# Per-token scales spread to all partitions by two transfers through memory in place of a matmul of ones with a diagonal

## What is computed

```python
def rmsnorm(x, g):
    y = x * rsqrt(mean(x * x, axis=-1) + RMS_EPS)
    return y * g

# first block: mixers, then the feed-forward part
x = x + concatenate([y_a, y_b, y_c]) @ w_out
h = rmsnorm(x, norm_ffn)
up = dwconv3(h @ ffn_w_up, ffn_conv_w, ffn_conv_b)     # 2048 -> 2 * 5632, width-3 convolution over tokens
gate, val = split(up, 2)
x = x + (silu(gate) * val) @ ffn_w_down                # 5632 -> 2048
x = rmsnorm(x, norm_final)

# second block: attention with a forget gate, then an MLP
h = rmsnorm(x, norm_g[0])
q, k, v, f_pre = split(h @ fox_w_in)                   # 2048 -> 3 * 2048 + 16
...
x = x + rmsnorm(attention @ fox_w_out, norm_g[1])
x = x + rmsnorm(square(relu(rmsnorm(x, norm_g[2]) @ mlp_w1)) @ mlp_w2, norm_g[3])
```

## Time and profile before

| | |
|---|---|
| median of 3 runs | 2156.41 us (2156.26 to 2156.44) |
| span of the profiled execution, first to last instruction | 2154.2 us |
| mean granted TensorE clock | 0.999 |
| PE busy | 2146.4 us, 100% of the span as printed |
| DVE / ACT / POOL busy | 1304.1 / 1010.3 / 63.3 us |
| share of PE in the chain that ended last | 98% |
| DMA | 412.43 MB, mean 191 GB/s |

### The profile page before, as it was taken

How to read it: one execution, slowest core, us unless ns; L and a number is a source line. 1 busy time by engine, 2 the same in 40 slices (tenths; PEclk the granted TensorE clock), 3 DMA queues, 4 the chain that set the end, 5 groups by cost and what they waited for, 6 DMA issues and landing times.

```text
span 2154.2 us, 28093 instructions
## 1 busy us (share of the span) xinstructions
PE 2146.4 (100%) x11745; PEld 1862.1 (86%) x11745; DVE 1304.1 (61%) x1610; ACT 1010.3 (47%) x1188; POOL 63.3 (3%) x85
## 2 busy tenths in 40 slices
PE   9999999999999999999999999999999999999999
PEld 7888888888888888888898889888888888888887
DVE  7968557777777775444755665466555555444445
ACT  6444446555545554444655444445434334444443
POOL 3030000000000000000001010000000000000000
PEclk9999999999999999999999999999999999999999
DMA  9655656565655555555566555547666665555552
GB/s 343 212 169 176 217 188 201 182 195 189 196 189 184 194 176 203 192 194 193 166 211 201 157 177 189 198 142 215 186 187 194 186 189 193 195 195 196 192 192 105
DMA packets 269214, 412.43 MB, mean 191 GB/s; under 512 B 7013, under 2 KB 247589, under 8 KB 250400
## 3 DMA queue, kind: packets, MB, share of 16 engines
q1 hardware_dynamic: 266080, 398.48, 56.8%
q0 software_dynamic: 2432, 11.75, 1.5%
q10 hardware_dynamic: 576, 0.40, 0.1%
HBM read 408.49 MB, written 2.11 MB: 191 GB/s over the span
## 4 chain that ended last, share of the span: by engine, by line
PE 98%; DMA 1%; ACT 1%; DVE 0%; SPq 0%; issue 0%; ACTq 0%; DVEq 0%
PE bank L1586 35%; PE bank L1599 18%; PE bank L1647 11%; PE bank L1648 11%; PE bank L1652 11%; PE bank L1589 2%; PE bank L1601 2%; PE bank L1590 2%; PE bank L1481 1%; DMA M<-in_xt 1%; PE bank L1673 0%; PE bank L1670 0%; PE bank L1671 0%; PE bank L1564 0%; PE bank L1531 0%; PE bank L1517 0%
## 5 line engine op out<-in xcount | busy, mean ns | idle before, releaser
L822 DVE TENSOR_TENSOR wlo<-raw,whi 128x2048 fp32r<-128x2048 f32 (+1 forms) x372 | 852.5, 2294 | 762.1 <-ACT whi L496 762.0
L496 ACT ACTIVATE whi<-raw 128x2048 fp32r<-128x2048 f32 (+1 forms) x371 | 710.2, 1916 | 777.9 <-PE bank L1652 421.3
L1586 PE MATMUL bank<-hh,whi 128*128 128x512 f32 x3360 | 807.3, 392 | 0.1
L1586 PEld LDWEIGHTS bank<-hh,whi 128*128 128x128 f32 x3360 | 618.2, 188 | 123.3 <-issue 0.9
L1599 PEld LDWEIGHTS bank<-hh,wlo 128*128 128x128 f32 x3360 | 430.6, 191 | 16.9 <-DVE wlo L822 0.6
L1599 PE MATMUL bank<-hh,wlo 128*128 128x256 f32 x3360 | 436.0, 283 | 0.2 <-DVE wlo L822 0.2
L1647 PE MATMUL bank<-whi,hh 128*128 128x512 f32 x1072 | 417.3, 389 | 0.0
L1648 PE MATMUL bank<-whi,hh 128*128 128x512 f32 x1072 | 417.1, 389 | 0.0
L1652 PE MATMUL bank<-wlo,hh 128*128 128x512 f32 x1072 | 264.8, 389 | 0.0
L1652 PEld LDWEIGHTS bank<-wlo,hh 128*128 128x128 f32 x1072 | 201.2, 188 | 41.9
L1647 PEld LDWEIGHTS bank<-whi,hh 128*128 128x128 f32 x1072 | 201.2, 188 | 41.8 <-DVE M L894 0.2
(11 more groups left out here) (249 smaller groups left out, 935.8 us busy)
## 6 DMA issues: line engine op xcount, KB each, us to landing
raw<-in_mlp_w SPq DMA_DIRECT2D x128, 1024.0 KB, 5.5
raw<-in_ffn_w_up SPq DMA_DIRECT2D x88, 1024.0 KB, 5.1
raw<-in_ffn_w_down SPq DMA_DIRECT2D x44, 1024.0 KB, 4.8
raw<-in_fox_w_in SPq DMA_DIRECT2D x32, 1024.0 KB, 5.3
raw<-in_w_in SPq DMA_DIRECT2D x31, 1024.0 KB, 5.6
raw<-in_fox_w_in SPq DMA_DIRECT2D x16, 1032.0 KB, 5.4
raw<-in_w_out SPq DMA_DIRECT2D x16, 1024.0 KB, 4.8
raw<-in_fox_w_out SPq DMA_DIRECT2D x16, 1024.0 KB, 4.7
```

The costliest lines, as they stand in the source:

```text
L496: e.activation(whi[i % RING][:, 0:n], raw[i % RAW][:, 0:n], ACT.Copy).then_inc(s_hi, 1)
L822: e.tensor_tensor(wlo[i % RING][:, 0:n], raw[i % RAW][:, 0:n], whi[i % RING][:, 0:n].bitcast(F), ALU.subtract).then_inc(s_lo, 1)
L1586: e.matmul(bank[b][:, :], wh[:, k, s], hh[:, kk, :], start=kk == 0, stop=False)
```

## The change

For `r_up` and `rtot` the diagonal, the matmul and the copy are gone. Instead POOL writes the two columns of 128 words to a row of `cum` in HBM (two transfers), waits for both, and reads the row back to all 128 partitions of `rb` (one transfer). DVE waits for that transfer where it waited for the matmul. The early use (`rstd`) stays.

```diff
-    51: [("up_r", 0), ("split", 55)], 53: [("up_r_out", 0)], U_DOWN - 2: [("early", 1)],
-    182: [("gains", 0)], 183: [("gain_squares", 0)], 184: [("both_r", 0)], 185: [("ahead", 188)], 186: [("both_r_out", 0)],
+    51: [("up_r", 0), ("split", 55)], U_DOWN - 2: [("early", 1)],
+    182: [("gains", 0)], 183: [("gain_squares", 0)], 184: [("both_r", 0)], 185: [("ahead", 188)],
...
+            def to_all(n, r):
+
+                for h in range(2):
+                    e.dma_start(cum[n:n + 1, h * P:h * P + P].rearrange("o p -> p o"), r[:, h:h + 1]).then_inc(s_rdram, 16)
+                e.wait_ge(s_rdram, 32 * (n + 1))
+                e.dma_start(rb[:, :], cum[n, :].partition_broadcast(P)).then_inc(s_rall, 16)
...
             e.dma_start(gfr, A["gf_row"].partition_broadcast(P)).then_inc(s_gainf, 16)
+            e.wait_ge(s_rcp, 3)
+            to_all(0, r_up)
             e.wait_ge(s_xg, 2)
+            e.wait_ge(s_rr, 3)
+            to_all(1, rtot)
             e.wait_ge(s_unit, U_FOX + 4)
...
                 e.tensor_tensor(rtot, r_b, r_a, ALU.mult).then_inc(s_rr, 1)
-                e.wait_ge(s_rr, 3)
-                diagonal(rtot)
...
                         root(3, SS[0], 1.0 / D, RMS_EPS, r_up)
-                        e.wait_ge(s_rcp, 3)
-                        diagonal(r_up)
...
                 if g == 0:
-                    spread_out(2)
+                    e.wait_ge(s_rall, 16)
                 conv(kind, j, b, group_done(U_UP, g))
...
                 if (kind, j) == ("k", 0):
-                    spread_out(3)
+                    e.wait_ge(s_rall, 32)
                     out_of_psum("q", 0, group_done(U_FOX, 0))
...
-                    elif what == "up_r_out":
-                        e.wait_ge(s_lx, 32)
-                        spread(2)
-                    elif what == "both_r_out":
-                        e.wait_ge(s_lx, 48)
-                        spread(3)
...
                     elif what == "sums":
+                        e.wait_ge(s_lx, 48)
                         e.wait_ge(s_gt, 12)
```

More of the change, by code:

```diff
@@ L273, in two_block_program @@
         s_ss, s_red, s_rr, s_dg, s_bc, s_rb = (sem(n) for n in ("s_ss", "s_red", "s_rr", "s_dg", "s_bc", "s_rb"))
+        s_rdram, s_rall = sem("s_rdram"), sem("s_rall")
         s_gainf, s_gain1, s_gain3, s_xt, s_xg, s_yg = (sem(n) for n in ("s_gainf", "s_gain1", "s_gain3", "s_xt", "s_xg", "s_yg"))
@@ L859, in diagonal, with spread_out @@
                     e.tensor_scalar(dg[:, h, :], ident[:, :], r[:, h:h + 1], None, ALU.mult).then_inc(s_dg, 1)
-            def spread_out(n):
-                e.wait_ge(s_bc, n)
+            def spread_out():
+                e.wait_ge(s_bc, 1)
                 e.tensor_copy(rb[:, :], bank[7][:, 0:T]).then_inc(s_rb, 1)
-                e.wait_ge(s_rb, n)
+                e.wait_ge(s_rb, 1)
             def root(n, sums, scale, eps, dst):
@@ L1245, in vector @@
             convolved("v", 0, 2, group_done(U_IN, 1))
-            spread_out(1)
+            spread_out()
             times_r("x1", 0)
@@ L1440, in turn_two, with spread @@
                         t.then_inc(s_xt, 1)
-            def spread(n):
-                e.wait_ge(s_dg, 2 * n)
+            def spread():
+                e.wait_ge(s_dg, 2)
                 e.matmul(bank[7][:, 0:T], ones, dg[:, :, :].rearrange("p h t -> p (h t)"), start=True, stop=True).then_inc(s_bc, 1)
@@ L1486, in side @@
                     if what == "spread":
-                        spread(1)
-                    elif what == "up_r_out":
-                        e.wait_ge(s_lx, 32)
-                        spread(2)
-                    elif what == "both_r_out":
-                        e.wait_ge(s_lx, 48)
-                        spread(3)
+                        spread()
                     elif what == "filter1":
@@ L1700, in last_rows @@
                 e.wait_ge(s_yg, 8 + 8)
-                e.wait_ge(s_dg, 7)
+                e.wait_ge(s_dg, 3)
                 for n, c in enumerate(BY_DIAGONAL):
@@ L1744, in tensor @@
             rows(1, [up_free(n_up + 1, 0), up_free(n_up + 1, 1), up_free(n_up + 2, 0), up_free(n_up + 2, 1), up_free(n_up, 0), up_free(n_up, 1),
-                     None, (s_rb, 2)])
+                     (s_lx, 32), (s_lx, 32)])
             def fox_free(g, n):
```

## The result

| | before | changed |
|---|---|---|
| median | 2156.26 us (2156.17 to 2156.44, 5 runs) | 2175.88 us (2173.63 to 2177.04, 5 runs) |
| ratio, with 95% interval | | 1.0089 [1.0079, 1.01] |
| span of the profiled execution | 2154.2 us | 2174.1 us |
| granted TensorE clock | 0.999 | 0.996 |
| waits of PE in the two places | 0 | 8.1 + 7.3 us |

A forecast was written before the change was run, and what follows sets the result against it. PE was taken as the bound from end to end; 0.86 us saved against waits of 0.2 and 0.5 gave -0.16 us, so 2156.41 became 2156.25, say 2156.3 us. The range was 2155.4 to 2160.5.

The forecast's parts named there:

- PE is the bound; the two matmuls are worth 0.86 us: Whole span: PE bounds end to end; each removed spread saves 0.43 us, in up and attention projections, together 0.86.
- The form of L: Both places, finished factor to `rb` landed: POOL notices 0.29, issue 0.54, write 4.7, read 4.5; L = 10.0, range 8.3 to 12.8.
- The write, 4.7 us: Both places: second write's issue to the read's issue, 4.7 us, from `fox_b2` landing in 4.4 plus 0.3; low 3.88.
- my upper end of 7.3: Both places: highest price for the write, from the 3 KB `skip_row`, which landed in 7.0 us.
- writes of single words are slow: Rival, 12%: POOL's wait for both writes lengthens; write 7.3, read 4.9, L 13.0, net 5.8, time 2162.2 us.
- 2L - 20.2: Net change in us once L exceeds 9.8 (up) and 9.5 (attention), each microsecond costing PE one per place; passes 4.3 at 12.2.
- The read, 4.5 us: Both places: read of the row to 128 partitions lands in 4.5 us, like `mask`; low 3.6, high 4.7.
- The free lateness, 3.3 to 4.0 us in the up projection and L = 9.5 in the attention projections: Lateness before PE waits: up 3.3 (unit 57) or 4.0 (unit 56), allowing L = 9.8; attention, q0's bank, L = 9.5.
- a wait for `whi` of 56: Up projection: this wait would show the line of work wrong; unit 57 was expected, with under 1 us.
- The clock isn't priced: PE's clock: no cost for a fall, since it stayed at 1.00 with 1.24 us idle in ten; shorter waits expected.
- DVE holds up POOL's transfers: Rival, 3%: both places, DVE's `wlo` instructions delay the second write's descriptors; PE waits 4.9 and 5.1, time 2165.6 us.

The follow-up runs named there:

- experiment 7: Changed kernel, same six transfers, but groups 0 and 1, q0 and k0 are emptied first and multiplied by `rb` later: 2155.51 us, ratio 0.9996.
- experiment 3: Changed kernel, but each write sends a 512-byte row of ones from one partition instead of a column of 128 words: 2159.02 us, ratio 1.0014.
- probes: Kernel before, with single transfers of various piece sizes and spacings added that nothing waits for; 128 words side by side landed in 9.4 to 10.0 us.
- Experiment 5: Kernel before, without any transfer, but the matmul for `r_up` two units later, behind unit 55 instead of 53: 2165.43 us.
- Experiment 2: Changed kernel, but words written 8 bytes apart, 2 KB read to every partition and every second word copied to `rb` by DVE: 2169.22 us.
- second kernel of experiment 3: Changed kernel with row writes, but the read to 128 partitions takes an input row instead of the row just written: 2159.11 us.

## Why the prediction was wrong, step by step

- **PE is the bound; the two matmuls are worth 0.86 us**: right. In the changed kernel the low parts of units 53 and 54 start 5.57 apart (335.90 and 341.47) instead of 6.00. With the waits out of the way (experiment 7) the median is 0.8 below before, which the interval doesn't separate from nothing. (Of PE's waits before, the 1.1 us at line 1612 that I counted as one wait is two, of which the longer took 0.9; nothing hangs on it.)
- **The form of L**: right. POOL's 0.28 and 0.54, then write, then read, just as the chain shows.
- **The write, 4.7 us**: the step that failed. It took 11.2 and 9.5 from its issue to the read's, above my upper end of 7.3. The 4.7 is what the write of a row took at the first place (experiment 3). I took the duration from `fox_b2` and called a read with rows of 128 bytes the nearest row of the trace. The probes say what was wrong with that: rows don't matter, bytes don't, but a write whose pieces start 4 bytes apart isn't like anything that the kernel had done before. The rival "writes of single words are slow" named the mechanism, its place and the point from which it decides; it was given 12% and, with a wrong bound for the write (and 4.9 for the read, which no row shown gives), 2162.2. Its 2L - 20.2, with the two measured L, is 15.5, and the measured waits less the 0.86 are 14.5.
- **The read, 4.5 us**: too low by 2. It measured 6.7 and 6.4 there, and 6.5 and 6.2 with an input row. I had taken the landing of `mask`, beside which one load of weights was pending at a time, and here there were two (experiment 3). By itself this term would have cost what experiment 3 measured, 2.7 us, and stayed within the range.
- **The free lateness, 3.3 to 4.0 us in the up projection and L = 9.5 in the attention projections**: right. In the up projection DVE starts at 351.06, 12.15 late when the run's own shift of 0.41 is taken off; less the 4.0 for `whi` of unit 56 that is 8.15, and 8.06 were measured. The sign that the prediction gave for this line of work being wrong, a wait for `whi` of 56, was a wrong sign: unit 57 has the smaller margin (3.3 against 4.0), but PE comes to unit 56 first, so any lateness above 4.0 shows there, and only the difference of 0.7 is left for unit 57. In experiment 3 both are seen, 1.57 and 0.40. In the changed kernel the 0.7 went by unseen, since unit 56 ran 1.96 us longer. In the attention projections 17.0 - 9.5 = 7.5, and 7.3 were measured. Experiment 5 has the same relation without transfers.
- **The clock isn't priced**: a second step that failed, and it followed from the first. It rested on 1.24 us of idle time. Behind waits of 8.1 and 7.3 us PE came back at 1.2 GHz, and that cost 1.96 and 2.63 us, 4.6 of the 19.6. Experiment 2 had waits of 4.8 and 4.3 us and lost 2.1 and 2.5 behind them; the single-word rival, with waits of 3.2 and 3.5, left the term out too.
- **DVE holds up POOL's transfers**: not supported. In experiment 3, with DVE and POOL in the same order, the writes take 4.4 and 3.0.
- **What the Trainium skill states.** "DMA: Bandwidth & Descriptors", section "Anatomy of one DMA — SWDGE (gpsimd) path", gives about 2.0 us and bytes over 436 GB/s; the runs don't agree, no probe landed sooner than 4.2 us, and the fastest of the added transfers in any run, a row of 512 bytes in the second kernel of experiment 3, took 2.9. The same page of the Trainium skill, section "Specifications", has read-modify-write below 512 bytes; here pieces of 12 to 64 bytes landed as fast as those of 512 (4.2 to 4.8), so by itself that rule doesn't name the case. The slow writes are those whose pieces start 4 or 8 bytes apart.

## What to carry to other kernels

When an operation has no like in the trace, ask which of its properties none of the known rows shares (here a write, of words, side by side), and let the upper end of its price go where the wait would hurt, not only to the slowest row at hand. A column of words that goes to HBM is better written in pieces at least 12 bytes apart, or as a row; for 12 bytes and more the evidence is the probes alone, since in the kernel itself only 8 bytes apart and a row were run. And a long transfer in place of a short matmul is harmless when what waits for it has nothing urgent queued behind it on its engine: moving the wait was worth 20 us here. Quickening the write was worth 7 with words 8 bytes apart and 17 with a row, and the row left out the factors' values, which would first have to be brought onto one partition. A wait of PE can cost more than itself: behind waits of 4.3 to 8.1 us the lower clock cost another 1.8 to 2.8, behind one of 1.6 us 0.1.

## What the runs showed of the hardware that I had not expected

- 128 words written side by side to HBM land in 9.4 to 10.0 us in the probes, 16 words in 4.2, and 128 words 16 bytes apart in 4.3.
- While they are under way, the loads of the weights are slow too: 1 MB takes 14.4 us (write from POOL's queue) or 12.0 (from ACT's) instead of 5.1, and the DMA engines look busy in the profile (0.81 of the time) while they move 60 GB/s.
- Words read side by side from HBM land in 4.5 us; it is a matter of writes.
- PE came back from waits of 4.3 to 8.1 us at a granted clock near 0.5; the high part that followed took 5.5 to 6.7 us instead of 3.65 or 3.84, and the low part behind it ran at its usual pace again.
